# A three-block network on one core: expert results added to their tokens in DRAM by indexed DMAs

## The chip, the cores and the metric

The kernel runs on one core of one Trainium2 chip. The metric is the device time of one launch in microseconds (us): a median of 3149.73 over three runs (3148.05 to 3154.68). The profile is of one execution.

## The reference

A first block (recurrence, attention, feed-forward) is followed by a second block of two layers. Each layer of the second block ends in a mixture of experts with fixed capacity. The layer in question, the first, runs it for 512 latent tokens and, with the same weights, for 256 context tokens:

```python
def ec_moe(h, w_router, w_gate, w_up, w_down):
    bsz, n_tok, d = h.shape                       # d = 1024
    cap = EC_CAPACITY * n_tok // N_EXPERTS        # 64 of 512, 32 of 256; 16 experts
    aff = jax.nn.softmax(jnp.einsum('bnd,de->bne', h, w_router).astype(jnp.float32), axis=-1)
    g, idx = lax.top_k(jnp.swapaxes(aff, 1, 2), cap)
    xs = jax.vmap(lambda hb, ib: hb[ib])(h, idx)
    hid = jax.nn.silu(jnp.einsum('becd,edf->becf', xs, w_gate)) * jnp.einsum('becd,edf->becf', xs, w_up)
    ye = jnp.einsum('becf,efd->becd', hid, w_down) * g[..., None].astype(h.dtype)
    return jax.vmap(lambda yb, ib: jnp.zeros((n_tok, d), h.dtype).at[ib.reshape(-1)].add(yb.reshape(-1, d)))(ye, idx)
```

Around it, in each layer: `x = layer_norm(ALPHA * x + g2 * ec_moe(modulate(x, ...), ...))`, and the same for the context with its own modulation. A token can be chosen by several experts, so its line is a sum over them.

## The kernel before

`layer` calls `experts` (L2459) and then `norm_tiles` (L1883), once for each layer; both stand as stages with a crossing of all engines between them. All is float32. In `experts` the sixteen experts are taken as eight pairs (0 to 7). Their weights, 24 chunks of 1 MB for a pair, come through a ring of 8 slots and, in the first layer, 3 lent ones (the tile names `ring` and `tokens_b`); SP issues them in one order, each as soon as the chunk before it in its slot has been used (`Stream.issue`, L257).

`route` picks the tokens. `aff` holds the gates, `pos` the slot of each token at each expert. For each pair:

- `choose` (DVE) compares `pos` with a row of numbers and makes one-hot tables `choL`, `choC` (token by slot; L for latents, C for context). `list_slots` (PE, L2513 and L2516) multiplies them by the tokens' numbers, which gives the token of each slot; `take_index` (DVE) turns these into integers, and POOL fetches the tokens' lines from DRAM with two indirect DMAs (L2776, L2778). This runs two pairs ahead for the list and one pair ahead for the lines.
- `turn_rows` (PE) transposes the lines into PSUM, and ACT's `modulate` (L2744) scales them into `xsL`, `xsC`.
- `matrix` is one of the three products (gate, up, down) over 8 chunks: `latents` (L2558), then `context` (L2566), in groups of four chunks. The order on PE is: first product, second product, then what this text calls the **gap**, then the third product.
- In the gap PE does `turn_gates` (L2588, L2590), which transposes one-hot tables that DVE had multiplied by the gates (`gate`), `turn_hidden` (L2601), `turn_rows` for the next pair, `list_slots` for the pair after that, and `scatter` of the pair before (L2617): 12 products of the turned gate tables with that pair's results `yeL`, `yeC`, each added into `moe` (the tile name `tokens_a`) by DVE (L2706), with two PSUM banks in turn. The third product writes the banks that `turn_rows` filled, so it waits for ACT's `modulate`.
- After the third product DVE multiplies the result by the modulation row `growL`, `growC` (L2727, L2729), which gives `yeL`, `yeC`.

After pair 7 its scatter stands alone at the end, and `norm_tiles` starts with the statistics of `moe`, tile by tile (L1942). `moe` starts as ALPHA times x, made by ACT in `route`. The second layer has no context part (`C` and `G` are 0) and does not take this path.

## Time and profile before

| What | Value |
|---|---|
| median of three runs | 3149.73 us |
| the profiled execution | 3148.66 us, span 3146.8 us |
| PE busy | 2842.6 us, 90% of the span |
| PE weight loads | 1625.4 us, 52% |
| DVE / ACT / POOL busy | 1060.2 / 676.8 / 28.7 us |
| mean granted clock of PE | 0.948 |
| DMA | 569.42 MB, mean 181 GB/s |
| L2617, PE, the scatter's products (latents, both layers) | 256 records, 122.4 us busy |

Times are us from the start of the span. A float32 matmul has two records on PE. "x8" counts records or instructions merged into one row. PEclk is the granted clock of TensorE as a share of 2.4 GHz, so that 0.50 is 1.2 GHz. The DMA share is the mean busy share of the core's 16 DMA engines; it can pass 1 slightly in a short stretch. "Idle before" names what ended an engine's idle time. The busy time of overlapping records on PE is that of their union.

### The profile page before, as it was taken

Reading aid. Unit: us, or ns where it says so; the run is one execution under the profiler, and the core shown is the slowest. Engines: PE = TensorE matmul, PEld = TensorE weight load, DVE = VectorE, ACT = ScalarE, POOL = GpSimd, SP = SyncE. Lnnn points to the kernel's source line nnn. Section 1 sums busy time; section 2 is a strip of 40 time slices with the busy share of each in tenths; the row PEclk is TensorE's granted clock in tenths of the full one; section 3 lists DMA queues with packets and bytes.
Section 4 is the critical chain, followed back from the end, with each engine's and each line's share of the span. In section 5 each row is a group of like instructions: output and inputs, shape, how many; then the busy total and the mean of one; then the engine's idle time right before and its main releaser. Section 6 shows DMA issues by size and latency. Waiting matters only on the chain. (4 is left out here: it accounts for less than half of the span.)

```text
span 3146.8 us, 36640 instructions
## 1 busy us (share of the span) xinstructions
PE 2842.6 (90%) x15568; PEld 1625.4 (52%) x15568; DVE 1060.2 (34%) x2192; ACT 676.8 (22%) x1399; POOL 28.7 (1%) x45
## 2 busy tenths in 40 slices
PE   6998889899999689999489999999599995999996
PEld 5775655588864356774233333333277743433432
DVE  2513445132320227485501111111653753111213
ACT  3212225211100221471321111110211723100100
POOL 0010000000000000000000000000000000000000
PEclk9999979999999889999789999999799997999998
DMA  3227660122222121000368888887131004999995
GB/s 131 74 88 261 236 269 35 67 80 73 75 87 80 62 61 54 28 2 34 127 244 331 331 331 331 331 321 321 67 87 54 1 28 187 421 423 424 424 423 235
DMA packets 96904, 569.42 MB, mean 181 GB/s; under 512 B 24995, under 2 KB 25539, under 8 KB 31461
## 3 DMA queue, kind: packets, MB, share of 16 engines
q1 hardware_dynamic: 92852, 553.86, 45.1%
q0 software_dynamic: 3888, 13.22, 1.2%
q8 instruction: 123, 2.02, 0.3%
q14 instruction: 41, 0.33, 0.0%
HBM read 558.01 MB, written 9.03 MB: 180 GB/s over the span
## 5 line engine op out<-in xcount | busy, mean ns | idle before, releaser
L2558 PE MATMUL ps<-ring,xsL 128*64 128x512 f32 x1536 | 344.8, 600 | 9.6 <-ACTq L196 7.6
L1789 PE MATMUL ps<-hT,ring 128*128 128x257 f32 x1408 | 308.3, 381 | 1.6 <-PEq L1582 1.6
L1789 PEld LDWEIGHTS ps<-hT,ring 128*128 128x128 f32 x1408 | 268.0, 190 | 41.9 <-issue 1.9
L2558 PEld LDWEIGHTS ps<-ring,xsL 128*64 128x64 f32 x1536 | 109.7, 138 | 238.4 <-issue 221.2
L2721 DVE TENSOR_TENSOR hidL<-hidL,ps 128x1024 f32<-128x1024 f32 x16 | 19.5, 1221 | 515.6 <-PE ps L2566 312.9
L1752 PE MATMUL ps<-ring,actT 128*128 128x512 f32 x352 | 153.1, 598 | 7.0 <-PEq L1777 7.0
L2558 PE MATMUL ps<-ring,htL 128*64 128x512 f32 x616 | 140.0, 605 | 7.1 <-issue 3.8
L2751 ACT ACTIVATE hidL<-ps 128x1024 f32<-128x1024 f32 x16 | 16.4, 1023 | 603.3 <-PE ps L2566 368.2
L820 PE MATMUL ps<-hT,ring 128*128 128x264 f32 x640 | 143.8, 386 | 1.7 <-PEq L289 1.7
L2215 PE MATMUL ps<-tokens_a,ring 128*128 128x384 f32 x416 | 136.8, 491 | 4.9 <-PEq L384 4.9
L820 PEld LDWEIGHTS ps<-hT,ring 128*128 128x128 f32 x640 | 121.4, 190 | 23.2 <-issue 2.6
L2617 PE MATMUL ps<-yeL,gtL 128*128 128x512 f32 x256 | 122.4, 615 | 3.3 <-DVE yeC L2729 1.9
L2727 DVE TENSOR_TENSOR yeL<-ps,growL 128x1024 f32<-128x1024 f32 x16 | 19.6, 1224 | 289.3 <-PE ps L2566 171.3
L1752 PEld LDWEIGHTS ps<-ring,actT 128*128 128x128 f32 x352 | 67.5, 192 | 92.1 <-issue 92.1
L2215 PEld LDWEIGHTS ps<-tokens_a,ring 128*128 128x128 f32 x416 | 79.6, 192 | 60.9 <-issue 7.8
L2215 PE MATMUL ps<-tokens_b,ring 128*128 128x256 f32 (+1 forms) x416 | 103.6, 412 | 4.2 <-PEq L1909 4.2
L2333 DVE SCALAR_TENSOR_TENSOR z<-pad,cols,z 128x783 f32<-128x783 f32 (+1 forms) x120 | 101.9, 891 | 2.1
L601 ACT COPY probT<-ps 128x1280 f32<-128x1280 f32 (+5 forms) x80 | 81.1, 1013 | 69.2 <-PE ps L499 69.0
L2558 PEld LDWEIGHTS ps<-ring,htL 128*64 128x64 f32 x616 | 43.9, 139 | 99.2 <-issue 99.2
L2215 PEld LDWEIGHTS ps<-tokens_b,ring 128*128 128x128 f32 x416 | 80.8, 195 | 26.4 <-issue 5.3
L1834 DVE TENSOR_SCALAR conv<-raw,cols 128x512 f32<-128x512 f32 x44 | 19.4, 483 | 214.2 <-ACTq L196 214.2
L2566 PE MATMUL ps<-ring,xsC 128*32 128x512 f32 x768 | 88.8, 595 | 0.0
(492 smaller groups left out, 3893.9 us busy)
## 6 DMA issues: line engine op xcount, KB each, us to landing
ring<-in_w_exp SPq DMA_DIRECT2D x269, 1024.0 KB, 10.6
ring<-in_w SPq DMA_DIRECT2D x73, 1024.0 KB, 4.9
tokens_b<-in_w_exp SPq DMA_DIRECT2D x67, 1024.0 KB, 9.4
ring<-in_w_mod SPq DMA_DIRECT2D x48, 1024.0 KB, 5.2
h<-in_w_exp SPq DMA_DIRECT2D x16, 1024.0 KB, 14.5
tokens_a<-in_w_exp SPq DMA_DIRECT2D x16, 1024.0 KB, 15.2
lent<-in_w_exp SPq DMA_DIRECT2D x16, 1024.0 KB, 16.6
h<-in_x SPq DMA_DIRECT2D x2, 2048.0 KB
```

What stands on the lines that cost most here:

```text
L601: act.copy(probT[0:u["turn"], i % 2, 0:2 * nt, 0:u["n"]], T[0:u["turn"], 0:2 * nt, 0:u["n"]]).then_inc(pt_ready.sem, 1)
L820: mm = pe.matmul(ps[0:m, bank + h, 0:HALF1], lhs(c_), hT[:, c_, h * HALF1:(h + 1) * HALF1], start=c_ == 0, stop=c_ == KD - 1, skip_group_c ...
L1752: mm = pe.matmul(k.ps[:, 2 * j + half, :], actT[:, f, P * j:P * j + P], s[:, kk, half * BANK:(half + 1) * BANK], start=f == 0, stop=f == F ...
L1789: mm = pe.matmul(k.ps[:, 4 * (j % 2) + 2 * gv + h, 0:HALF], w(c_), hT[:, c_, FIRST + h * HALF:FIRST + (h + 1) * HALF], start=c_ == 0, stop ...
L1834: steps.free(dve.tensor_scalar(y, x, cw, None, ALU.mult))
L2215: mm = pe.matmul(ps[:, bank + h, 0:half], w(c_), uT[:, c_, h * half:(h + 1) * half], start=c_ == 0, stop=c_ == KD - 1, skip_group_check=True)
L2333: steps.free(dve.scalar_tensor_tensor(z[:, g, :], src, w, z[:, g, :], ALU.mult, ALU.add))
L2558: mm = pe.matmul(ps[HD * par:HD * par + HD, bank + half, :], lhsL(kk, par), weights(kk)[:, half, par, :], start=kk == 0, stop=kk == KD - 1 ...
L2566: mm = pe.matmul(ps[q:q + CAP_C, cbank, :], lhsC(kk, par), weights(kk)[:, half, par, :], start=kk == 0, stop=kk == KD - 1, skip_group_chec ...
L2617: pe.matmul(ps[:, MISC + half, :], lhsT, rhs, start=True, stop=True, skip_group_check=True).then_inc(scat.sem, 1)
L2721: dve.tensor_tensor(h[:, :], h[:, :], src, ALU.mult).then_inc(hid.sem, 1)
L2727: dve.tensor_tensor(yeL[:, :], psf[:, UB * BANK:(UB + 2) * BANK], growL[:, :], ALU.mult).then_inc(yes.sem, 1)
```

## The change

In the first layer the gate tables, their transposes and the scatter products are gone. The lists are made for more columns, so that each slot gets its token, its gate and, for the context, a second number: the product is with `table` (gates of both experts and the token's number) in place of the token's number alone, and some lists are made again for the odd expert, so that its results stand at partitions 0 to 63. `take_index` keeps integers and gates of all pairs. Behind the third product DVE multiplies by the slot's gate and the modulation row in one instruction. POOL adds the results to lines of `token_sums` in DRAM, four indirect DMAs for each pair: the even expert's latents and context, a wait for both, and the odd expert's (the two experts of a pair can have a token in common). `moe` is written to `token_sums` once at the start, and read back in six DMAs at the end; `norm_tiles` waits for each tile. The columns of PSUM that the context products write are ordered by expert now, which `growC` follows.

```diff
+                    if back and half == 0:
+                        dve.wait_ge(back[t].sem, back[t].of(16))
...
-            norm_tiles(k, ntq, x, summed=(moe, gb), to_next=(moe, by_channel_tile(b), k.mod[:, l + 1], 0))
+            norm_tiles(k, ntq, x, summed=(moe, gb), to_next=(moe, by_channel_tile(b), k.mod[:, l + 1], 0), back=k.back)
...
-                for t in range(NTL):
-                    pe.matmul(ps[:, MISC + 1, 256:257], choL[:, t, :, :].rearrange("p a s -> p (a s)"), c("token")[:, t:t + 1],
-                              start=t == 0, stop=t == NTL - 1, skip_group_check=True)
-                for t in range(2):
-                    mm = pe.matmul(ps[0:HD, MISC + 1, 257:258], choC[:, t, :, :].rearrange("p a s -> p (a s)"),
-                                   c("token")[:, NTL + t:NTL + t + 1], start=t == 0, stop=t == 1, skip_group_check=True)
-                mm.then_inc(listed.sem, 1)
+                if n >= 1:
+                    pe.wait_ge(indexed.sem, indexed.of(n))
+
+                def listing(m, at, lhs, lo, tiles, cols, first=0):
+                    for t in range(tiles):
+                        mm = pe.matmul(ps[first:first + m, MISC + 1, at:at + cols], lhs(t), table[:, lo + t, n, 3 - cols:3],
+                                       start=t == 0, stop=t == tiles - 1, skip_group_check=True)
+                    return mm
+                listing(P, 0, lambda t: choL[:, t, :, :].rearrange("p a s -> p (a s)"), 0, NTL, 3)
+                listing(HD, 3, lambda t: choL[:, t, 1, :], 0, NTL, 1)
+                for par in range(2):
+                    listing(CAP_C, 4, lambda t: choC[:, t, par, 0, :], NTL, 2, 1, CAP_C * par)
+                listing(P, 5, lambda t: choC[:, t, :, :, :].rearrange("p a h s -> p (a h s)"), NTL, 2, 3)
+                listing(HD, 8, lambda t: choC[:, t, 1, :, :].rearrange("p h s -> p (h s)"), NTL, 2, 1).then_inc(listed.sem, 1)
...
-                            q = HD * half + CAP_C * par
+                            q = HD * par + CAP_C * half
...
-                    if i == 1 and G:
-                        pe.wait_ge(indexed.sem, indexed.of(min(n + LEAD + 2, PAIRS)))
                     t, half = i // 2, i % 2
-                    if t < NTL:
-                        lhsT, rhs = gtL[:, n % 2, t, :], yeL[:, half * BANK:(half + 1) * BANK]
-                    else:
-                        b = slice(HD * half, HD * half + HD)
-                        lhsT, rhs = gtC[b, n % 2, t - NTL, :], yeC[b, :]
-                    pe.matmul(ps[:, MISC + half, :], lhsT, rhs, start=True, stop=True,
+                    pe.matmul(ps[:, MISC + half, :], gtL[:, n % 2, t, :], yeL[:, half * BANK:(half + 1) * BANK], start=True, stop=True,
...
-                turn_gates(n)
+                if not G:
+                    turn_gates(n)
                 turn_hidden(n)
                 if n + 1 < PAIRS:
                     if G:
                         turn_rows(n + 1)
                     else:
                         gather(n + 1)
-                pe.wait_ge(gts.sem, gts.of(n + 1))
-                if G and n + LEAD < PAIRS:
-                    list_slots(n + LEAD)
-                if n >= 1:
-                    scatter(n - 1)
+                if G:
+                    if n + LEAD < PAIRS:
+                        list_slots(n + LEAD)
+                else:
+                    pe.wait_ge(gts.sem, gts.of(n + 1))
+                    if n >= 1:
+                        scatter(n - 1)
...
+                for half in range(2 * C):
+                    is_slot(choC[:, :, :, half, :], pos, n, NTL, NT2, CAP_C)
...
+                got = ps[:, MISC + 1, :]
+                steps.free(dve.tensor_copy(index[0:HD, n, 0:3], got[0:HD, 2:5]))
+                steps.free(dve.tensor_copy(index[HD:P, n, 0:1], got[HD:P, 2:3]))
+                steps.free(dve.tensor_scalar(index[0:HD, n, 3:5], got[0:HD, 7:9], 2.0, c("low_half")[0:HD, :], ALU.mult, ALU.add))
+                for par in range(2):
+                    b = slice(HD * par, HD * par + HD)
+                    steps.free(dve.tensor_copy(gates[b, n, 0:1], got[b, par:par + 1]))
+                    steps.free(dve.tensor_copy(gates[b, n, 1:2], got[b, 5 + par:6 + par]))
                 steps.tell(indexed.sem)
+
+            def ended(n):
+
+                dve.wait_ge(used.sem, used.of(PAIR_CHUNKS * n + 24))
+                yL = psf[:, UB * BANK:(UB + 2) * BANK]
+                if G:
+                    if n >= 1:
+                        dve.wait_ge(summed.sem, summed.of(64 * n))
+                    dve.scalar_tensor_tensor(yeL[:, :], yL, gates[:, n, 0:1], growL[:, :], ALU.mult, ALU.mult).then_inc(yes.sem, 1)
+                    dve.scalar_tensor_tensor(yeC[:, :], ps[:, CU, :], gates[:, n, 1:2], growC[:, :], ALU.mult,
+                                             ALU.mult).then_inc(yes.sem, 1)
+                else:
+                    dve.tensor_tensor(yeL[:, :], yL, growL[:, :], ALU.mult).then_inc(yes.sem, 1)
...
+                steps.free(dve.tensor_copy(table[:, :, :, 0:2], aff[:, :, :].rearrange("p t (n a) -> p t n a", a=2)))
+                steps.free(dve.tensor_copy(table[:, :, :, 2], c("token").unsqueeze(2).to_broadcast([P, NT2, PAIRS])))
...
-                pool.wait_ge(sg["kept"].sem, sg["kept"].of(0))
-                for n in range(PAIRS):
+                def fetch(n):
                     pool.wait_ge(indexed.sem, indexed.of(n + 1))
                     if n >= 1:
                         pool.wait_ge(xs_turned.sem, xs_turned.of(PARTS * n))
                     pool.indirect_dma_start(rows[:, 0, :], None, k.rows[:, :],
-                                            bass.IndirectOffsetOnAxis(index[:, 0:1], 0)).then_inc(fetched.sem, 16)
+                                            bass.IndirectOffsetOnAxis(index[:, n, 0:1], 0)).then_inc(fetched.sem, 16)
                     pool.indirect_dma_start(rows[0:HD, 1, :], None, k.rows[:, :],
-                                            bass.IndirectOffsetOnAxis(index[0:HD, 1:2], 0)).then_inc(fetched.sem, 16)
+                                            bass.IndirectOffsetOnAxis(index[0:HD, n, 2:3], 0)).then_inc(fetched.sem, 16)
+
+                def sum_up(n):
+                    for par in range(2):
+                        b = slice(HD * par, HD * par + HD)
+                        if n >= 1 or par >= 1:
+                            pool.wait_ge(summed.sem, summed.of(32 * (2 * n + par)))
+                        pool.wait_ge(yes.sem, yes.of(PARTS * n + 1))
+                        pool.indirect_dma_start(k.sums[:, :], bass.IndirectOffsetOnAxis(index[0:HD, n, par:par + 1], 0), yeL[b, :],
+                                                None, compute_op=ALU.add).then_inc(summed.sem, 16)
+                        pool.wait_ge(yes.sem, yes.of(PARTS * n + 2))
+                        pool.indirect_dma_start(k.sums.rearrange("t (h d) -> (t h) d", h=2),
+                                                bass.IndirectOffsetOnAxis(index[0:HD, n, 3 + par:4 + par], 0), yeC[b, :], None,
+                                                compute_op=ALU.add).then_inc(summed.sem, 16)
+
+                pool.wait_ge(sg["kept"].sem, sg["kept"].of(0))
+                fetch(0)
+                pool.dma_start(k.sums.rearrange("(t p) d -> p t d", p=P), moe[:, :, :]).then_inc(begun.sem, 16)
+                pool.wait_ge(begun.sem, begun.of(16))
+                for n in range(1, PAIRS):
+                    fetch(n)
+                    sum_up(n - 1)
+                sum_up(PAIRS - 1)
+                pool.wait_ge(summed.sem, summed.of(64 * PAIRS))
+                for t in range(NT2):
+                    pool.dma_start(moe[:, t, :], k.sums[P * t:P * t + P, :]).then_inc(k.back[t].sem, 16)
```

PE from the end of the second product of pair 1 to its third product, before (`gatL`, `gatC` the gate tables, `rows` the fetched lines, `choL`, `choC` the one-hot tables, `htL` the hidden values for the third product):

```order
L2566 MATMUL ps<-ring,xsC 32x512 x16
L2588 MATMUL ps<-const,gatL 128x128 x4
L2590 MATMUL ps<-const,gatC 128x128 x2
L2601 MATMUL ps<-const,hidL 128x128 x8
L2601 MATMUL ps<-const,hidC 128x128 x4
L2524 MATMUL ps<-const,rows 128x128 x8
L2528 MATMUL ps<-const,rows 128x64 x8
L2513 MATMUL ps<-const_54,choL 128x1 x4
L2516 MATMUL ps<-const_54,choC 64x1 x2
L2617 MATMUL ps<-yeL,gtL 128x512 x8
L2617 MATMUL ps<-yeC,gtC 128x512 x4
L2558 MATMUL ps<-ring,htL 64x512 x4
```

and now:

```order
L2571 MATMUL ps<-ring,xsC 32x512 x16
L2601 MATMUL ps<-const,hidL 128x128 x8
L2601 MATMUL ps<-const,hidC 128x128 x4
L2536 MATMUL ps<-const,rows 128x128 x8
L2540 MATMUL ps<-const,rows 128x64 x8
L2522 MATMUL ps<-table,choL 128x3 x4
L2522 MATMUL ps<-table,choL 64x1 x4
L2522 MATMUL ps<-table,choC 32x1 x4
L2522 MATMUL ps<-table,choC 128x3 x2
L2522 MATMUL ps<-table,choC 64x1 x2
L2563 MATMUL ps<-ring,htL 64x512 x4
```

The turned gate tables (L2588, L2590) and the scatter (L2617) are gone from the gap, and the six matmuls of the list (4 and 2) have become sixteen (4, 4, 4, 2 and 2).

POOL's queue at the end of the stage, before (waits in brackets):

```order
L2776 DMA rows<-token_rows,index 128x1024 [waits xs_turned,indexed]
L2778 DMA rows<-token_rows,index 64x1024
L2776 DMA rows<-token_rows,index 128x1024 [waits xs_turned,indexed]
L2778 DMA rows<-token_rows,index 64x1024
L2506 UNCONDITIONAL_BRANCH
```

and now:

```order
L2787 DMA rows<-token_rows,index 128x1024 [waits xs_turned,indexed]
L2789 DMA rows<-token_rows,index 64x1024
L2798 DMA token_sums<-yeL,index 768x1024 [waits yes,summed]
L2801 DMA token_sums<-yeC,index 1536x512 [waits yes]
L2798 DMA token_sums<-yeL,index 768x1024 [waits yes,summed]
L2801 DMA token_sums<-yeC,index 1536x512 [waits yes]
L2798 DMA token_sums<-yeL,index 768x1024 [waits yes,summed]
L2801 DMA token_sums<-yeC,index 1536x512 [waits yes]
L2798 DMA token_sums<-yeL,index 768x1024 [waits yes,summed]
L2801 DMA token_sums<-yeC,index 1536x512 [waits yes]
L2815 DMA tokens_a<-token_sums 128x1024 [waits summed]
L2815 DMA tokens_a<-token_sums 128x1024 x5
```

The fetch for pair 7 stands ahead of the sums of pair 6, and the sums of pair 7 and the six reads of the tiles stand behind them. The fetch for each later pair stands behind all four sums of an earlier one in the same queue.

## Rows read from the trace of the kernel before

**Rows 1.** The page, part 2: mean GB/s of all DMA in 40 equal slices of the span.

```profile
GB/s 131 74 88 261 236 269 35 67 80 73 75 87 80 62 61 54 28 2 34 127 244 331 331 331 331 331 321 321 67 87 54 1 28 187 421 423 424 424 423 235
```

**Rows 2.** Stretches, us from the start: length, busy us and count by engine, PEclk, DMA share, GB/s.

```profile
1885.97:1966.63 80.66, 80.12 (x455) 27.17 (x454) 15.09 (x26) 9.15 (x22) 1.84 (x2) 1.00 0.81 323
1906.90:1949.50 42.60, 42.60 (x261) 12.59 (x257) 4.81 (x10) 1.51 (x2) 0.00 (x0) 1.00 0.99 397
1949.50:1955.20 5.70, 5.16 (x51) 4.66 (x47) 1.82 (x2) 4.02 (x10) 0.00 (x0) 1.00 1.01 425
1636.00:1641.00 5.00, 1.35 (x13) 1.25 (x12) 0.21 (x2) 4.88 (x15) 1.84 (x2) 0.90 1.02 429
```

**Rows 3.** Timeline, PE, gap of pair 4: start us, length, line, operation, records, [idle before].

```profile
1949.50 0.66 PE L2588 MATMUL ps<-const,gatL 128*128 128x128 f32 x4
...
1950.91 1.09 PE L2601 MATMUL ps<-const,hidL 128*128 128x128 f32 x8 [0.54 <-DVE hidL L2721]
...
1953.89 1.05 PE L2513 MATMUL ps<-const,choL 128*128 128x1 f32 x8
1954.87 0.39 PE L2516 MATMUL ps<-const,choC 128*64 128x1 f32 x4
1955.20 7.70 PE L2617 MATMUL ps<-yeL,gtL 128*128 128x512 f32 x16
...
1966.63 0.65 PE L2558 MATMUL ps<-ring,htL 128*64 128x512 f32 x2
```

**Rows 4.** Timeline, ACT, the same gap.

```profile
1956.47 2.47 ACT L2744 ACTIVATE xsC<-ps,mod 128x64 f32<-128x64 f32 x8
```

**Rows 5.** Timeline, PE, gap of pair 0 and the third product behind it.

```profile
1631.59 0.66 PE L2588 MATMUL ps<-const,gatL 128*128 128x128 f32 x4
...
1641.17 8.17 PE L2558 MATMUL ps<-ring,htL 128*64 128x512 f32 x24 [3.82 <-issue]
...
1665.15 1.08 PE L2558 MATMUL ps<-ring,xsL 128*64 128x512 f32 x4
```

**Rows 6.** Timeline, all engines, gap of pair 7.

```profile
2190.20 0.66 PE L2588 MATMUL ps<-const,gatL 128*128 128x128 f32 x4
...
2193.65 0.59 ACT L2763 COPY htC<-ps 128x512 f32<-128x512 f32 x1
...
2204.32 0.65 PE L2558 MATMUL ps<-tokens_b,htL 128*64 128x512 f32 x2
```

**Rows 7.** Timeline, all engines, opening of the stage.

```profile
1569.59 1.87 PE L2513 MATMUL ps<-const,choL 128*128 128x1 f32 x8 [1.82 <-DVEq L196]
...
1571.38 0.59 PE L2516 MATMUL ps<-const,choC 128*64 128x1 f32 x4
1572.01 0.16 DVE L2698 CAST index<-ps 128x1 int32<-128x1 f32 x1 [2.54 <-PE ps L2516]
...
1573.12 1.02 POOL L2776 DMA_INDIRECT rows<-token_rows,index  x1 [46.89 <-DVEq L196]
...
1574.44 0.92 POOL L2778 DMA_INDIRECT rows<-token_rows,index  x1 [0.30 <-issue]
...
1578.71 1.97 PE L2524 MATMUL ps<-const,rows 128*128 128x128 f32 x8 [2.89 <-DMA rows<-token_rows,index]
```

**Rows 8.** Timeline, DVE, end of the stage and the first row of the next.

```profile
2225.63 1.22 DVE L2727 TENSOR_TENSOR yeL<-ps,growL 128x1024 f32<-128x1024 f32 x1 [20.52 <-PE ps L2566]
...
2240.29 0.69 DVE L1942 BATCH_NORM_STATS2 stats<-tokens_a 128x6 f32<-128x512 f32 x1 [0.54 <-PEq L2506]
```

**Rows 9.** DMA issues (KB each, median us to landing), landing of token rows (DMA_INDIRECT), POOL issue.

```profile
lent<-in_w_exp SPq DMA_DIRECT2D x16, 1024.0 KB, 16.6
...
token_rows<-tokens_b POOLq DMA_DIRECT2D x6, 512.0 KB, 2.9
...
DMA to landing us min/median/max: 4.2/6.2/7.5
...
L2017 POOL DMA_DIRECT2D token_rows<-tokens_b x6 | 3.2, 532 | 1286.9 <-ACT tokens_b L2000 1286.9
```

More of the change, by code:

```diff
@@ L114, in constants @@
     first = [n for i, n in enumerate(parts) if i < first_only and n not in both]
-    second = ["iota", "token", "band"]
+    second = ["iota", "token", "low_half", "band"]
     inputs = [n for n in parts if n not in both and n not in first and n not in second]
@@ L1880, in by_channel_tile, with norm_tiles @@
     return buf[:, :].rearrange("p (k t) -> p k t", k=KD)
-def norm_tiles(k, nt, x, residual=None, summed=None, to_next=None, store=None, keep=None):
+def norm_tiles(k, nt, x, residual=None, summed=None, to_next=None, store=None, keep=None, back=None):
     nc, sg = k.nc, k.sig
@@ L2491, in experts @@
         rows = sb("rows", [P, 2, D])
-        index = sb("index", [P, 2], mybir.dt.int32)
+        index = sb("index", [P, PAIRS, 5], mybir.dt.int32)
+        gates = sb("gates", [P, PAIRS, 2])
+        table = sb("table", [P, NT2, PAIRS, 3])
     with ExitStack() as ctx:
         route(k, k.alloc(ctx), (xsL[:, :, :, :].rearrange("p k a s -> p (k a s)"), htL[:, :, :].rearrange("p k s -> p (k s)"),
-                                gtL[:, :, :, :].rearrange("p a t q -> p (a t q)"), hidL, yeL), uT, aff, pos, ntq, x, mod, moe, growL, growC)
+                                rows[:, 0, :] if G else gtL[:, :, :, :].rearrange("p a t q -> p (a t q)"), hidL, yeL), uT, aff, pos, ntq, x, mod, moe, growL, growC)
     if not C:
@@ L2540, in gather @@
                 mm.then_inc(xs_turned.sem, 1)
-                if C:
-                    for ch in range(KD):
-                        for t in range(2):
-                            mm = pe.matmul(ps[:, CU, ch * HD:(ch + 1) * HD], u[:, NTL + t, ch * P:(ch + 1) * P],
-                                           choC[:, t, :, :].rearrange("p a s -> p (a s)"), start=t == 0, stop=t == 1,
-                                           skip_group_check=True)
-                    mm.then_inc(xs_turned.sem, 1)
             def matrix(n, m, bank, cbank, lhsL, lhsC):
@@ L2584, in turn_gates @@
                     pe.wait_ge(added.sem, added.of(N_SC * (n - 1)))
-                if G:
-                    pe.wait_ge(indexed.sem, indexed.of(min(n + LEAD, PAIRS)))
                 for t in range(NTL):
                     mm = pe.transpose(ps[:, MISC, t * P:(t + 1) * P], gatL[:, t, :, :].rearrange("p a s -> p (a s)"), c("ident"))
-                for t in range(2 * C):
-                    mm = pe.transpose(ps[:, MISC + 1, t * P:(t + 1) * P], gatC[:, t, :, :, :].rearrange("p h a s -> p (h a s)"),
-                                      c("ident"))
                 mm.then_inc(gtr.sem, 1)
@@ L2684, in gate @@
                 is_slot(gatL[:, :, :, :], pos, n, 0, NTL, CAP_L)
-                for half in range(2 * C):
-                    is_slot(gatC[:, :, half, :, :], pos, n, NTL, NT2, CAP_C)
                 steps.join()
                 times_gate(gatL[:, :, :, :], n, 0, NTL, CAP_L)
-                for half in range(2 * C):
-                    times_gate(gatC[:, :, half, :, :], n, NTL, NT2, CAP_C)
                 steps.tell(gatd.sem)
@@ L2715, in _ @@
                     choose(n + LEAD)
-                gate(n)
+                if not G:
+                    gate(n)
                 for part in range(PARTS):
@@ L2784, in experts @@
     used.close(PAIR_CHUNKS * PAIRS)
-    for s in (choice, gatd, gtr, gts):
-        s.close(PAIRS)
+    choice.close(PAIRS)
     for s in (xs_turned, xs_, silu, hid, htr, hts, yes):
@@ L2792, in experts @@
         fetched.close(32 * PAIRS)
-    scat.close(N_SC * PAIRS)
-    added.close(N_SC * PAIRS)
+        begun.close(16)
+        summed.close(64 * PAIRS)
+    else:
+        for s in (gatd, gtr, gts):
+            s.close(PAIRS)
+        scat.close(N_SC * PAIRS)
+        added.close(N_SC * PAIRS)
 def route(k, sb, spare, uT, aff, pos, ntq, x, mod, moe, growL, growC):
@@ L2866, in _ @@
                 act.wait_ge(row_made.sem, row_made.of(i + 1))
-                steps.free(act.copy(*row_of(i)))
+                dst, src = row_of(i)
+                if row_jobs[i][0] == 0:
+                    steps.free(act.copy(dst, src))
+                else:
+                    for q in range(CAP_C * row_jobs[i][1], P, 2 * CAP_C):
+                        steps.free(act.copy(dst[q:q + CAP_C, :], src[q:q + CAP_C, :]))
             act.wait_ge(made.sem, made.of(2))
@@ L2990, in program @@
         k.rows = nc.dram_tensor("token_rows", (T2, D), F32).ap()
+        k.sums = nc.dram_tensor("token_sums", (T2, D), F32).ap()
+        k.back = [Signal(ctx.enter_context(nc.semaphore(f"back{t}"))) for t in range(NT2)]
         k.b_mod = sb("b_mod", [P, LAYERS, 6 * KD])
```

55 lines of the change are left out of this document (25 added, 30 removed).

## The prediction

> **What bounds the kernel now.** I read the page's slices first, then the stretches of the first expert stage (about 1568 to 2240 us), then the timeline of one gap. In the stage PE is busy 80.12 of 80.66 us from one third product to the next, at the full clock; DMA is busy 0.81 of that time, and 0.99 of it while the products run [rows 2]. So PE bounds the stage and the weight stream follows with some room. The second layer's experts later run at 421 to 424 GB/s for five slices [rows 1]; that stretch is bound by its transfers, which start from a full ring, so an earlier start moves it as a whole and a gain made before it isn't lost there.
>
> A pair's three products take 80.66 less the gap of 17.13 (1949.50 to 1966.63, [rows 3]), that is 63.5 us, or 21.2 each, and aren't touched. In the gap the scatter's products run from 1955.20 to 1966.63, 11.4 us [rows 3]. But PE couldn't have gone on at 1955.20: the third product needs ACT's scaling of the next lines, which ends at 1956.47 + 2.47 = 1958.94 [rows 4]. Pair 0 shows the gap without a scatter: 1631.59 to 1641.14, 9.55 us, with 3.82 us idle at its end [rows 5], for the same reason.
>
> **The gaps.** Pairs 1 to 5: 17.13 becomes 9.55, 7.58 less each, 37.9 in all. Turning the gate tables was hidden already: PE starts on the hidden values at 1950.91, released by DVE [rows 3], so removing it gives nothing. The longer list is hidden too. Warm, a record of the old list took 1.05/8 = 0.13 us at 128 columns and 0.39/4 = 0.10 at 64 [rows 3]; the new one has 12 records of 128, 12 of 64 and 8 of 32 (priced as 64), 3.5 us in place of 1.4, and from 1953.89 it ends near 1957.4, before ACT does. If this cover were gone it would cost 2.1 us a gap. Pair 6 has no list: from 1949.50 to 2190.20 [rows 3, 6] are three gap starts, 240.7 = 3 x 63.5 + 2 x 17.13 + 15.9, so its gap is 15.9 and saves 6.3. Pair 7 has neither lines nor list and waits for the hidden values alone: 2193.65 + 0.59 = 2194.24, and the product goes at about 2194.3 in place of 2204.32 [rows 6], 10.0 less. Pair 0 has no scatter to lose. Together **-54.2 us**.
>
> DVE's adds go with the scatter, and DVE waited anyway. The new scaling by the gate replaces a multiply of the same size, with 21 us before the next user of its PSUM banks.
>
> **The clock.** In pair 0 the granted share falls to 0.90 in 1636 to 1641 [rows 2], around the idle 3.82 us. The next 24 records take 8.17 us [rows 5], and the third product 1665.15 - 1641.14 = 24.0 us against 21.2: a fall to 1.2 GHz costs 2.8 us. In the gap of pair 4 the first 5.7 us hold transposes, a list and waits and stay at 1.00 [rows 2]; behind them comes the scatter with 512 columns. The change takes this scatter away in each gap. Between the last transposes and the third product there will then be 3.5 us of list with 1 to 3 columns and 1.5 us of idling (pair 6: about 5 us idle). No row shows a list this long, so the cost of a gap lies between 0 and 2.8 us. A saving is possible as well: pair 0 would get its 2.8 back if the list keeps the clock up. I take 2.8, as the state of PE (next to no columns for 5 us) is nearest to pair 0's, for pairs 1 to 6: **+16.8 us**. At 0 the forecast would be 3108, and with pair 0's gain 3106.
>
> The Trainium skill, TensorE: Matmul & The Clock Gate (PE-mode transpose), says that transposes don't count as busy for the clock in the way that matmuls do. The stretch of pair 4 that kept 1.00 through its transposes speaks against an immediate effect; by the page all gaps would dip, which is the sum as I take it.
>
> **The opening.** This runs on the critical path with PE at half clock. Ahead of the first list stand two copies for `table` (DVE, about 0.4 together, estimated from the small casts) and one more comparison (0.3). The old list took 1.87 + 0.59 = 2.46 us [rows 7]; at its 0.234 and 0.148 us a record the new one takes 5.8: +3.3. Seven conversions replace two, each at most 0.16 long and overlapped [rows 7]: +0.4. So the first fetch goes 4.4 later than 1573.12. Its lines would land near 1583.1 in place of 1578.71, but PE is then still at the second list, which has to stand ahead of the transposes: 4.7 later and 5.8 long, to 1583.9. **+5.2 us**; bounds 3 (lists as short as warm ones) to 8. The write of `moe` to DRAM (3 MB) stands behind the fetch, and its wait holds up only the second fetch, which has over 40 us.
>
> **The end of the stage.** Before: the last results from 2225.63, then 12 products and adds, and the next stage's first row at 2240.29 [rows 8]. Now: results of the latents at about 2226.95; POOL follows 0.3 later. A round is two issues, 1.02 + 0.30 to the second's start, and its landing. Two rounds are in series. Landing of an adding DMA isn't in the trace. A fetch of lines took 4.2 to 7.5 us [rows 9]; a sum reads its destination and writes it. Low end: 4.2, a round of 5.5. High end: 16.6, the landing of a 1 MB chunk in a long queue [rows 9], a round of 17.9. I take 7.5, the slowest fetch, so 8.8 a round. Then 2227.2 + 17.6 + 0.6 for two reactions; six reads at 0.53 on POOL [rows 9], 3.2, since the crossing waits for POOL's issuing; 0.5 for the crossing: 2249.1. The first tile, issued near 2245.4 and 2.9 landing [rows 9], is there by then. **+8.8 us**, bounds +2.2 and +27.
>
> The Trainium skill, DMA: Bandwidth & Descriptors (Anatomy of one DMA), fits a POOL-issued DMA with about 2 us plus its bytes at 436 GB/s. Its figure for a round's 0.39 MB would be 2.9 us of landing, and the whole sum would be 3116; the fetch's 4.2 at the least is above it.
>
> **In the middle of the stage** the sums are hidden in time: they start with a pair's end, and the next fetch in POOL's queue is needed 42 us (two products) and 3 later, against two rounds of 8.8 and a fetch of 7.5.
>
> Sum: -54.2 + 16.8 + 5.2 + 8.8 = -23.4. From the profiled execution's 3148.66 this gives **3125 us**; that execution is 1.1 below the median of the runs shown.
>
> **Rivals.**
>
> - A: the list keeps the clock up in most gaps. For: the 1.00 over 5.7 us of transposes and list. Against: pair 0, where the same work plus idling fell. 3148.66 - 54.2 + 5.2 + 8.8, with dips in pair 6 alone (+2.8) and pair 0's own gone (-2.8): 3108.
> - B, slower than before: the adding transfers hold the 16 DMA engines, and weights arrive late. DMA is busy 0.81 x 80.66 = 65.3 us a pair; the new pair is 73.1 us, which leaves 7.8 for two rounds. If a round holds the engines for H us, the deficit is 2H - 7.8 a pair, seven times, less about 18 us that seven chunks ahead in the ring cover once; the end of the stage costs 2H - 6.2. With -54.2 + 5.2 the total is zero at H = 8.0. At H = 10 it is +32: 3181. For: nothing in the trace shows what an addition costs an engine. Against: 0.39 MB at the 397 GB/s of [rows 2] is 1 us, 2 with the read of the destination.
> - C: the landing of a round is at its high end but leaves the engines free: 18 us more at the stage's end, 3143. It would look like a small gain or none.
> - D: the change doesn't shorten the gaps because another wait stands there, as the wait for the fetch behind the sums in POOL's queue. It would take rounds above 18 us each; that is B or C grown further.
>
> **Chances.** The forecast 0.48, A 0.27, C and mixtures near no change 0.13, B and D 0.12. The forecast's own range is 3115 to 3134. The range that should hold 8 in 10 is 3103 to 3146. About 0.2% (6 us) can be told from no change: faster 0.82, same 0.07, slower 0.11.
>
> **What would show it.** Right: gaps of pairs 1 to 6 of 9.5 us, ending with ACT's last scaling; PEclk of 0.5 for some us behind them; third products of 24.0 us; a fetch landing well ahead of its transposes; first row of the next stage about 23 us behind the last result. Wrong: idle time of PE before a product put down to a chunk; a gap set by the list or the fetch; first product and opening more than 8 us later; a last round beyond 18 us.

## The result, and the profile after

| What | before | after |
|---|---|---|
| median of four runs each | 3152.20 us (3148.05 to 3156.02) | 3132.36 us (3128.35 to 3137.96) |
| ratio, 95% interval | | 0.9939, 0.9917 to 0.9961 |
| the profiled execution | 3148.66 us, span 3146.8 | 3137.96 us, span 3136.1 |
| mean granted clock of PE | 0.948 | 0.932 |

The change saves 19.8 us of the median; the sum of the forecast was 23.4 less than the profiled execution (3148.66 to 3125). A later run of the same changed kernel gave 3129.0 us against 3151.27, ratio 0.9926 (0.9909 to 0.9942).

The profiled execution of after is the longest of its four. It reaches the changed stage late: the last result of the router's preparation (DVE's `pos`) starts at 1577.15 us, and at 1567.80 before. In the eight traces of the experiments below, whose first block is the same, it starts between 1566.30 and 1574.82 (1571.64 for the same kernel), so this is a spread between executions. The stage is therefore counted from the end of that `pos`, 0.26 us behind its start, in both traces, to the first row of the next stage. A gap is counted here from the start of DVE's `hidL`, which both kernels have, to the third product, and the third product of pair 7 to the start of `yeL`:

| Part of the stage, us | before | after | difference | forecast |
|---|---|---|---|---|
| `pos` to the first product (opening) | 18.25 | 22.47 | +4.2 | +5.2 |
| first and second product of pair 0 | 45.41 | 45.03 | -0.4 | 0 |
| eight gaps, counted from `hidL` | 124.1 | 70.0 | -54.1 | -54.2 |
| eight third products | 172.35 | 184.66 | +12.3 | +16.8 |
| `yeL` of pair 7 to the next stage's first row | 14.65 | 32.17 | +17.5 | +8.8 |
| whole stage | 672.23 | 651.84 | -20.4 | -23.4 |

The first two products of pairs 1 to 7 take 42.49 us each in both. With -20.4, the 9.35 us of late arrival and 0.3 behind the stage, 3148.66 becomes the 3137.96 measured.

The gap of pair 1 in the trace of after (timeline, PE: start, length, line, operation, records, idle before), which answers to [rows 3]:

```profile
1721.89 1.09 PE L2601 MATMUL ps<-const,hidL 128*128 128x128 f32 x8 [1.34 <-DVE hidL L2734]
1722.82 0.60 PE L2601 MATMUL ps<-const,hidC 128*128 128x128 f32 x4
1723.26 1.04 PE L2536 MATMUL ps<-const,rows 128*128 128x128 f32 x8
1724.22 0.71 PE L2540 MATMUL ps<-const,rows 64*128 64x64 f32 x8
1724.86 1.61 PE L2522 MATMUL ps<-table,choL 128*128 128x3 f32 x16
1726.40 1.16 PE L2522 MATMUL ps<-table,choC 128*32 128x1 f32 x16
1730.06 3.68 PE L2563 MATMUL ps<-ring,htL 128*64 128x512 f32 x8 [2.50 <-issue]
```

The scatter is gone, the list takes 1.61 and 1.16, and PE then idles 2.50 us for ACT's scaling. The next eight records take 3.68 us; eight take 1.94 at the full clock. The stretches of the same place (length, then busy us and count of PE, PEld, DVE, ACT, POOL, then PEclk, DMA share, GB/s) answer to [rows 2]:

```profile
1726.00:1730.00 4.00, 1.56 (x24) 1.43 (x23) 0.89 (x7) 3.79 (x12) 0.00 (x0) 0.74 1.01 422
1729.00:1733.00 4.00, 2.94 (x8) 1.11 (x10) 0.00 (x0) 0.92 (x4) 0.00 (x0) 0.50 1.01 422
1733.00:1737.00 4.00, 4.00 (x16) 1.29 (x14) 0.00 (x0) 0.00 (x0) 0.00 (x0) 0.79 0.21 84
```

The clock stands at 1.2 GHz (0.50) as the third product begins and comes back within 1733 to 1737. The end of the stage (timeline, all engines), which answers to [rows 8]:

```profile
2197.07 1.28 DVE L2705 SCALAR_TENSOR_TENSOR yeL<-ps,gates,growL 128x1024 f32<-128x1024 f32 x1 [23.46 <-PE ps L2571]
...
2199.10 1.41 POOL L2798 DMA_INDIRECT token_sums<-yeL,index  x1 [54.29 <-DVE yeC L2706]
2200.81 1.41 POOL L2801 DMA_INDIRECT token_sums<-yeC,index  x1 [0.30 <-issue]
2209.45 1.41 POOL L2798 DMA_INDIRECT token_sums<-yeL,index  x1 [7.22 <-DMA token_sums<-yeC,index]
2211.16 1.41 POOL L2801 DMA_INDIRECT token_sums<-yeC,index  x1 [0.30 <-issue]
2215.59 3.32 POOL L2815 DMA_DIRECT2D tokens_a<-token_sums  x6 [3.02 <-DMA token_sums<-yeC,index]
...
2229.24 1.28 DVE L1945 BATCH_NORM_STATS2 stats<-tokens_a 128x6 f32<-128x512 f32 x2 [30.22 <-PEq L2511]
```

POOL has issued its last read at 2218.91, and the next stage begins 10.33 us later. The core's DMA engines are at rest from about 2226 (DMA share 0.78 in 2224 to 2226, 0.01 in 2226 to 2227). DVE's wait is put down to PE's sequencer, the crossing; but PE had nothing to do since 2197, so the name is not that of the culprit.

The page's row of GB/s, which answers to [rows 1]:

```profile
GB/s 132 66 95 241 225 258 80 54 81 81 68 87 80 73 65 41 41 2 27 134 235 334 353 364 356 343 342 345 104 88 54 2 40 189 417 423 424 423 423 233
```

The stage's slices have 334 to 364 GB/s where they had 321 to 331: the same weights in less time, and the sums. The second layer's experts stream at 417 to 424 as before, so what the first layer gained was kept.

### The profile page after: what moved, and what is told of

Its sections match the earlier page's. It is cut to its first block and busy times, and to the rows that moved or that the text cites. A ratio compares the mean times of both kernels' runs of the same rounds, so it can differ in the third digit from the quotient of the medians.

```text
span 3136.1 us, 36393 instructions
## 1 busy us (share of the span) xinstructions
PE 2779.8 (89%) x15488; PEld 1614.1 (51%) x15488; DVE 984.7 (31%) x2098; ACT 671.0 (21%) x1385; POOL 80.4 (3%) x84
## 5 line engine op out<-in xcount | busy, mean ns | idle before, releaser
L2563 PE MATMUL ps<-ring,htL 128*64 128x512 f32 x616 | 149.6, 639 | 20.6 <-issue 17.4
L1810 ACT COPY raw<-ps 128x514 f32<-128x514 f32 x44 | 23.7, 590 | 269.8 <-PE ps L1790 269.8
L1926 PE MATMUL ps<-const,tokens_a 128*128 128x128 f32 x80 | 17.8, 397 | 70.0 <-ACT tokens_a L2003 70.0
```

The lines of the kernel that those rows point to most:

```text
L1810: steps.free(act.copy(halves(raw[:, j % 2, gv, :]), k.ps[:, b:b + 2, 0:HALF]))
L1926: mm = pe.transpose(k.ps[:, 4 + 2 * (s % 2) + c_ // 4, (c_ % 4) * P:(c_ % 4 + 1) * P], u[:, s, c_ * P:(c_ + 1) * P], k.c("ident"))
L2563: mm = pe.matmul(ps[HD * par:HD * par + HD, bank + half, :], lhsL(kk, par), weights(kk)[:, half, par, :], start=kk == 0, stop=kk == KD - 1 ...
```

## Experiments

Two open questions led them. The clock theory says that third products are longer because PE does too little in the gap; its rival, that the adding transfers slow them. The queue theory says that the end waits until POOL's DMA queue is empty; its rivals, that additions land slowly or that reading the tiles back takes the time. Each ratio is against runs of the kernel before on the same chip, and "stage" is counted as in the table above.

**after again.** The changed kernel, unchanged, as a base.

> The changed kernel as it is, timed again beside the others. The profile of its first execution stood 10 us late before the changed stage was reached, so the stage itself gained some 20 us there. Theory S (the stage alone changed; the 10 us ahead of it are the spread between executions, in the first block, which the change does not touch): a ratio to the kernel before of 0.992 to 0.995, pair periods of 75.1 to 75.7 us, and ahead of the stage an offset to the kernel before that varies from execution to execution. Rival U (something in the change slows the first block): the stage is reached 9 to 10 us late again.

3129.0 us (3125.02 to 3133.33), ratio 0.9926 (0.9909 to 0.9942). Stage 651.12 against 651.84, all parts within 0.8 us of the table's. The stage's numbers repeat far better than the whole time, so the parts below are read from stages.

**fill.** PE gets products without a use behind the list, in the gap of pairs 0 to 6.

```diff
+            def fill(count):
...
+                for _ in range(count):
+                    pe.matmul(ps[:, MISC, :], c("ident"), growL[:, 0:BANK], start=True, stop=True, skip_group_check=True)
...
+                        fill(2)
+                    elif n + 1 < PAIRS:
+                        fill(5)
```

> The changed kernel with matmuls that nobody reads (512 columns, onto the PSUM bank that the scatter used) in the gaps: two behind the list of pairs 0 to 5, 1.7 us in an idle time of 2.5, and five in the gap of pair 6, 4.3 us in 5.1. Theory K (the third products lose 2.3 us each because the clock falls while PE has next to no columns to stream): gaps stay at 9.5 us, PEclk stays at 1.00, third products go from 23.5 to 21.2 us, 7 x 2.3 = 16 us less than the changed kernel in the same call. If two fillers are too few against 2.7 us of list, the clock falls in part of the gaps and 5 to 10 us are gained. Rival D (the first matmuls of the third product are slow because of the additions' transfers or of the operands, not of the clock): no change within 2 us, or slower by what the fillers push out.

3123.85 us (3120.18 to 3127.65), ratio 0.9908 (0.9888 to 0.9927), 5.2 less than after again. Stage 641.31, 9.8 less: the third products fall from 184.65 to 171.65, the gaps grow by 1.9 in sum (those of pairs 2 and 4 by 0.6 and 1.0), and the end of the stage took 1.3 more in this trace. The timeline of PE in its gaps of pairs 1, 2 and 4 (L2616 are the added products):

```profile
1722.55 1.98 PE L2616 MATMUL ps<-growL,const 128*128 128x512 f32 x4
1725.11 1.94 PE L2563 MATMUL ps<-ring,htL 128*64 128x512 f32 x8 [0.58 <-issue]
...
1795.66 3.24 PE L2616 MATMUL ps<-growL,const 128*128 128x512 f32 x4
1798.83 4.05 PE L2563 MATMUL ps<-tokens_b,htL 128*64 128x512 f32 x16
...
1942.89 3.68 PE L2616 MATMUL ps<-growL,const 128*128 128x512 f32 x4
```

In pair 1 the fill runs at the full clock and so does the product behind it: 1.94 us for eight records in place of 3.68. In pairs 2 and 4 the same four records take 3.24 and 3.68 us. The granted clock of these places (columns as above):

```profile
1795.00:1796.00 1.00, 1.00 (x9) 0.92 (x9) 0.20 (x2) 0.88 (x4) 0.00 (x0) 1.00 1.00 410
1796.00:1797.00 1.00, 1.00 (x3) 0.29 (x2) 0.69 (x6) 1.00 (x5) 0.00 (x0) 0.63 1.04 434
1942.00:1943.00 1.00, 1.00 (x16) 0.95 (x11) 0.01 (x1) 0.88 (x4) 0.00 (x0) 1.00 0.99 418
1943.00:1944.00 1.00, 1.00 (x2) 0.48 (x3) 0.89 (x7) 1.00 (x4) 0.00 (x0) 0.51 1.01 426
```

The clock was whole through the list and fell behind it, about 0.6 and 0.1 us into the fill (estimates from these shares), with PE busy. It fell in the fill of pairs 0 and 5 as well (2.80 and 2.77 us), so in four gaps of seven. This holds the clock theory, with one amendment: the 2.5 us of idling at the end of the gap aren't needed. What stood ahead of the fall in pairs 2 and 4 were the 1.34 us idle before the hidden values, transposes and the list of 1 to 3 columns. No run takes these 1.34 us away, so it isn't shown that the list would be enough without them. The four falls are also why the third products gave 13.0 us in place of some 16.

**noscatter.** The kernel before, with the scatter products and DVE's adds of the first layer left out and nothing in their place, so that the experts' results reach no token.

```diff
-                if n >= 1:
+                if n >= 1 and not G:
                     scatter(n - 1)
...
-            scatter(PAIRS - 1)
+            if not G:
+                scatter(PAIRS - 1)
```

> The kernel before with the scatter's products and adds of the first expert layer left out and nothing in their place: the expert results of that layer are not added to the tokens. It keeps the short list, the gate tables and their transposes, and has no additions in DRAM. Theory K: gaps of 9.5 us like the changed kernel's, third products of about 23.5 to 24 us with PEclk at 0.50 behind each gap. Sum: -54.2 for the gaps, +14 to +17 for the clock, -12 for the last scatter: 48 to 52 us less than the kernel before, 28 to 31 less than the changed kernel (opening 4, end of the stage 20, next to nothing for contention). Rival D: third products of 21.2 us, since no additions run, and 62 to 66 us less than the kernel before.

3095.05 us (3089.91 to 3098.53), ratio 0.9821 (0.9805 to 0.9836), stage 618.75. Third products 184.86 in sum, as long as those of after (184.66), without a single addition, and gaps of 9.46 us (9.61 in pair 6) against 9.44. PE behind its gap of pair 4, and the stretches there:

```profile
1941.60 9.11 PE L2558 MATMUL ps<-ring,htL 128*64 128x512 f32 x32 [3.83 <-issue]
```

```profile
1942.00:1946.00 4.00, 4.00 (x12) 1.21 (x10) 0.00 (x0) 0.00 (x0) 0.00 (x0) 0.54 0.66 228
1946.00:1950.00 4.00, 4.00 (x20) 1.38 (x18) 0.00 (x0) 0.00 (x0) 0.00 (x0) 1.00 0.00 0
```

So the longer third products are the clock's doing and the rival falls. It also prices the new way of summing: after's stage is 33.1 us longer (651.84 less 618.75), of which 4.2 stand in the opening (the longer lists) and 29.8 at the end (32.17 against 2.40). In the 597 us between, 28 additions and the six fetches queued behind them cost nothing that shows.

**best.** The conclusions put together: after with the fill, with two fill products ahead of the very first product, and with pair 7 summed by products with one-hot gate tables, as before. The reads of the tiles then stand behind the sums of pair 6, while pair 7 is computed.

```diff
+                fill(2)
...
-            if not G:
-                pe.wait_ge(yes.sem, yes.of(PARTS * PAIRS))
+            pe.wait_ge(yes.sem, yes.of(PARTS * PAIRS))
+            if G:
+                scatter_last()
+            else:
...
-                sum_up(PAIRS - 1)
-                pool.wait_ge(summed.sem, summed.of(64 * PAIRS))
+                pool.wait_ge(summed.sem, summed.of(64 * (PAIRS - 1)))
```

> A version meant to beat both: the changed kernel, with the fillers of the other run, two fillers more ahead of the first product, and with pair 7 combined by products with gate tables as before (its tokens' lines are read back from DRAM during pair 7, when the sums of pair 6 have landed), so that no addition in DRAM stands at the end of the stage. By theory K: 16 us less than the changed kernel for the clock in the gaps, 1 to 3 for the first product, and at the end of the stage 14.7 us from the last result to the first row of the next in place of 22.4, 7 to 8 less. Sum: 24 to 27 us less than the changed kernel, about 43 to 46 less than the kernel before. If the reading back (3 MB) makes a chunk of the weights late, part of the 8 is lost in pair 7.

3101.89 us (3097.59 to 3110.46), ratio 0.9842 (0.9823 to 0.9862), stage 621.35. This beats both kernels: 49 us less than before and 27 less than after again, measured together. Of the 29.8 us of the stage (against after again), 13.5 come from the third products (171.12), 16.1 from the end (15.36) and 2.5 from the first product of pair 0, which now starts at the full clock; the gaps give 2.4 back. Its timeline (POOL, then DVE) at the end:

```profile
2136.91 3.33 POOL L2864 DMA_DIRECT2D tokens_a<-token_sums  x6 [7.64 <-DMA token_sums<-yeC,index]
...
2181.07 1.22 DVE L2740 TENSOR_TENSOR yeL<-ps,growL 128x1024 f32<-128x1024 f32 x1 [23.45 <-PE ps L2572]
...
2196.43 1.29 DVE L1945 BATCH_NORM_STATS2 stats<-tokens_a 128x6 f32<-128x512 f32 x2 [0.53 <-PEq L2512]
```

POOL has issued its last read 41 us ahead of the last result, and 15.36 us behind it the next stage starts, near before's 14.65 [rows 8]. This run moves several things at once; the next ones separate the end.

**sp reads.** The six reads of the tiles are issued by SP, behind the weights, with the same wait for all sums; nothing else is changed.

```diff
-                for t in range(NT2):
-                    pool.dma_start(moe[:, t, :], k.sums[P * t:P * t + P, :]).then_inc(k.back[t].sem, 16)
...
+            if G:
+                sp.wait_ge(summed.sem, summed.of(64 * PAIRS))
+                for t in range(NT2):
+                    sp.dma_start(moe[:, t, :], k.sums[P * t:P * t + P, :]).then_inc(k.back[t].sem, 16)
```

> The changed kernel with the six reads of the tiles at the end issued from SP in place of POOL, everything else the same. In the changed kernel the first row of the next stage stands 13.6 us behind POOL's first read. Theory Q (the crossing waits for POOL's queue to run empty, so for all six reads, however each tile is waited for): SP's crossing doesn't wait for its transfers, and the next stage starts when the first tile is there, about 3 us behind the first read; from the last result to the first row 22 to 23 us in place of 32, and 9 to 10 us less than the changed kernel, a ratio to the kernel before near 0.989 to 0.990. Rival R (the reads themselves land late, behind each other or because HBM has to finish the sums): the first row stays at 30 to 32 us behind the last result.

3125.04 us (3116.62 to 3128.15), ratio 0.9907 (0.9892 to 0.9922), stage 642.45. Its timeline at the end:

```profile
2193.47 1.28 DVE L2705 SCALAR_TENSOR_TENSOR yeL<-ps,gates,growL 128x1024 f32<-128x1024 f32 x1 [23.45 <-PE ps L2571]
...
2195.50 1.41 POOL L2798 DMA_INDIRECT token_sums<-yeL,index  x1 [54.40 <-DVE yeC L2706]
...
2205.81 1.41 POOL L2798 DMA_INDIRECT token_sums<-yeL,index  x1 [7.18 <-DMA token_sums<-yeC,index]
...
2211.72 2.93 SPq L2821 DMA_DIRECT2D tokens_a<-token_sums  x6
2216.30 1.28 DVE L1945 BATCH_NORM_STATS2 stats<-tokens_a 128x6 f32<-128x512 f32 x2 [20.89 <-PEq L2511]
```

```profile
2218.00:2222.00 4.00, 0.00 (x0) 0.00 (x0) 3.89 (x7) 0.20 (x1) 0.00 (x0) 0.50 0.82 328
```

The two rounds are nearly the same. But from the end of the last issue (2214.65) to the first row it is 1.65 us, with the transfers still running (the stretch has 328 GB/s and DVE at work), against 10.33 when POOL had issued them. `yeL` to first row is 22.83 in place of 31.45 to 32.17. The queue theory holds and both its rivals fall for this part, since neither the additions nor the reads had become quicker. The six reads landed like this, in after and then here:

```profile
DMA to landing us min/median/max: 4.0/6.5/8.3
DMA to landing us min/median/max: 3.7/6.2/8.6
```

So in after the first tile could have been there at about 2220 (an estimate: the first issue at 2215.59 and 4.0), and DVE started at 2229.24. The raw trace has one more record on POOL, which the views leave out: a DRAIN, in after from 2217.70 to 2228.89, 11.19 us, which ends 0.35 us before the first row. It stands in sp reads too, 4.05 us long, to 2215.95, and again 0.35 before the first row, though no DMA of POOL was under way any more. In best, where the reads share the DMA engines with weights and take up to 25.0 us to land, it takes 27.78: its length goes with the landing. So the 1.65 us are not the price of a bare crossing either: POOL still ended last.

The Trainium skill, DMA: Bandwidth & Descriptors (SWDGE vs HWDGE vs iDMA), gives plain transfers to SP or ACT and keeps POOL for adding and irregular ones. This pair of kernels agrees, with 8.6 to 9.3 us for it at this place.

**split fill.** best, with the fill cut in two: one product between the two parts of the list and one behind it, since the clock fell within the list.

```diff
+                if n >= LEAD:
+                    fill(1)
...
-                        fill(2)
+                        fill(1)
```

> The version meant to beat both, with one of the two fillers of each gap moved into the middle of the list. In the filled kernel the fillers were slow from their first record in two of the seven gaps (3.2 and 3.7 us in place of 2.0), so the clock had fallen during the list. Theory K: the clock needs columns, and a list of 2.7 us has next to none; cut into 1.6 and 1.2 us it holds in all gaps, the gaps go to 9.5 and the third products to 21.2 us, 2 to 3 us less than the version before it in the stage. If a list of any length lets the clock fall once it is in the wrong place, some gaps stay at 10 us or more and the stage stays within 1 us.

A miss. 3113.62 us (3109.27 to 3115.47), ratio 0.9879 (0.9864 to 0.9894), stage 632.33, 11.0 more than best: 5.2 in the third products, 4.2 in the gaps, 1.4 at the end. In best the clock falls in four of the first seven gaps (pairs 0, 1, 3 and 5, with 2.65 to 3.63 us for the fill's four records in place of 1.98); here it is five. Timeline of PE, gap of pair 1 and then of pair 2 (L2518 the fill):

```profile
1716.09 1.66 PE L2518 MATMUL ps<-growL,const 128*128 128x512 f32 x2
1717.69 1.86 PE L2528 MATMUL ps<-table,choC 128*32 128x1 f32 x16
1719.47 2.07 PE L2518 MATMUL ps<-growL,const 128*128 128x512 f32 x2
...
1791.85 1.13 PE L2518 MATMUL ps<-growL,const 128*128 128x512 f32 x2
1792.91 1.16 PE L2528 MATMUL ps<-table,choC 128*32 128x1 f32 x16
1794.00 1.12 PE L2518 MATMUL ps<-growL,const 128*128 128x512 f32 x2
```

Pair 2 keeps its clock, with two records at 1.13; in pair 1 they take 1.66, so it fell about the start of the fill. The clock can fall behind the 1.34 us of idling, transposes and the first part of the list alone. The simple form of my theory, that more products closer together keep it up, isn't enough; what decides in which gap it falls stays open.

**plain.** after, with `compute_op=ALU.add` taken from the four indirect DMAs: lines are overwritten, not added to, with the same indices and the same bytes written, so the results aren't sums. One execution.

```diff
-                                                None, compute_op=ALU.add).then_inc(summed.sem, 16)
+                                                None).then_inc(summed.sem, 16)
...
```

> The changed kernel with plain indexed writes in place of additions: a token's line gets the result written last, so the experts' results are not summed. Same bytes written, no reading of the destination. In the changed kernel a round (latents and context) takes 10.2 to 11 us from the first issue to the next round's. Theory A (an addition costs the read of its destination and more issuing): issues of 0.9 to 1.0 us in place of 1.4, and rounds of 5.5 to 7 us, so 8 us less at the end of the stage; pair periods as before, since the rounds are hidden there. Rival P (rounds are set by fixed latency, not by adding): rounds of 9 us or more.

3124.24 us, stage 647.64. POOL's first two rounds, here and then in after:

```profile
1669.16 0.93 POOL L2798 DMA_INDIRECT token_sums<-yeL,index  x1 [77.00 <-DVE yeL L2705]
...
1677.70 0.89 POOL L2798 DMA_INDIRECT token_sums<-yeL,index  x1 [6.36 <-DMA token_sums<-yeC,index]
```

```profile
1679.83 1.49 POOL L2798 DMA_INDIRECT token_sums<-yeL,index  x1 [77.91 <-DVE yeL L2705]
...
1690.34 1.40 POOL L2798 DMA_INDIRECT token_sums<-yeL,index  x1 [7.29 <-DMA token_sums<-yeC,index]
```

An issue takes 0.89 in place of 1.41 us in the median and this round 8.5 in place of 10.5, of which 1.0 us is the two issues; the end of the stage is 28.92, 2.5 to 3.3 us shorter. Most of a round is what an indirect write costs, whether it adds or not.

**short list.** after, with the matmuls for the odd expert's second copies left out of the list, so that their indices aren't right; sizes and counts of the DMAs stay. `take_index` reads its numbers from the lists that are left. One execution.

```diff
-                listing(HD, 3, lambda t: choL[:, t, 1, :], 0, NTL, 1)
-                for par in range(2):
-                    listing(CAP_C, 4, lambda t: choC[:, t, par, 0, :], NTL, 2, 1, CAP_C * par)
...
-                listing(HD, 8, lambda t: choC[:, t, 1, :, :].rearrange("p h s -> p (h s)"), NTL, 2, 1).then_inc(listed.sem, 1)
...
```

> The changed kernel with six matmuls in the list in place of sixteen: the odd expert's results go to the tokens of the even one, and some gates are left from other slots, so that the sums are wrong in value and not in work. Expected: the opening (end of the routing's copy to the first product) goes from 22.5 back to 20 us, since two lists at half clock stood in it, one ahead of the fetch and one beside it; gaps unchanged at 9.5 us, as ACT ends them; third products between 23.2 and 24 us as before, since a shorter list leaves more idling in its place. If the list were what costs the clock, third products would come down to 21.2.

3127.5 us, stage 648.68. The opening is 20.39, 2.1 less. In the gaps the list takes 1.6 us and PE idles 3.71 (the eight records behind it take 3.68, as in after), and the third products sum to 183.92, 0.7 less than r1's 184.65: list or idling, the clock falls just the same.

## Why the prediction was right, and where it was wrong

- *The gaps, -54.2.* Right to 0.1 us in sum. From `hidL` the gaps of pairs 0 to 6 are 9.44 us and that of pair 7 is 3.96. Each ends with PE idling for ACT's last scaling, 2.50 us, and 5.13 in pair 6, which has no list. ACT's scaling was indeed what stood next behind the scatter.
- *The clock, +16.8.* Right in mechanism; the price of 2.8 us a gap was too high. Third products of pairs 1 to 6 take 23.47 down to 23.16 us against 21.18, which is 2.1 us each and 12.5 in all; the fall for every one of the seven gaps, and for no reason of DMA, is shown by noscatter. Pair 0's, from which the price was taken, was 23.97 before and 23.78 after: with the longer list its idle time shrinks from 3.82 us [rows 5] to about 2.5, and it loses nearly as much. Each later pair loses a little less than the one before it, with the same instructions in its gap; why was not tried.
- *The opening, +5.2.* 4.2, though the order of events was not as written. Either of the two first lists takes 4.6 us (2.81 and 1.84, overlapping), not 5.8: with 2.81 for the twelve records of 128 columns, which is the price taken, the twenty narrower ones took 0.09 each, not 0.148. Warm, it takes 2.7 and not 3.5, so it left PE idle for 2.5 us rather than 1.5. The second list was to end behind the landing of the lines; in after it ends at 1590.89, and the transposes wait 1.38 us more for the lines. So the 4.2 are 3.4 for a later fetch (POOL's issue 8.71 us behind the start of `pos`, 5.32 before; 4.4 forecast) and 0.8 more from its issue to the transposes. The end of the second list and the transposes (PE):

```profile
1589.05 1.84 PE L2522 MATMUL ps<-table,choC 128*32 128x1 f32 x16
1592.28 1.97 PE L2536 MATMUL ps<-const,rows 128*128 128x128 f32 x8 [1.38 <-DMA rows<-token_rows,index]
```

- *The end of the stage, +8.8.* The failed step, with 17.5. The two rounds, 17.6 and 0.6 for reactions, are 16.5 in fact (2199.10 to 2215.59), but not of one length: 10.35 and 6.14, the second with the DMA engines half busy (share 0.50 in 2210 to 2216). POOL's first issue waits for `yeC`, 0.75 us behind `yeL` and not 0.3. The six reads are 3.3 (forecast 3.2). What was mis-sized is "0.5 for the crossing", with its ground "since the crossing waits for POOL's issuing": it took 10.33, since it waits for what POOL has issued to land, and 3 to 4 us more (the DMA engines are at rest from about 2226, the first row is at 2229.24). sp reads shows it: 1.65 us there. The value lies within the bounds (+2.2 and +27), but these were made for the landing of the sums, so they held it for another reason. Its profile test, a first row about 23 us behind the last result, showed the miss: 32.17.
- *The middle of the stage.* Right: noscatter differs from after by less than 1 us outside the two ends. The fetches took longer than the 7.5 us allowed for them, 11.5 and 12.7 in the median (6.1 and 6.2 before) and 14.1 at most, and the 42 us hid that too. In after PE's waits in the stage (total us, times, longest) name no chunk at all:

```profile
PE ps L2563 <- issue: 19.9, 7, 5.1
PE ps L2601 <- DVE hidL L2734: 10.8, 8, 1.3
PE ps L2563 <- ACTq L197: 4.6, 1, 4.6
PE ps L2563 <- ACT htC L2775: 1.2, 1, 1.2
```

- *Rivals.* A (the clock stays up) is refuted by every gap. B (the additions hold the DMA engines) is refuted by the rows above. A round takes 10.5 us, more than the H of 8.0 that B needed, but as latency: the engines aren't held for it, or chunks would have been late. C asked for a round of 17.9; the longest is 11.2 (1755.73 to 1766.96). D would have shown as gaps above 9.5.

That the sum was off by 3.0 us only is luck, since misses of opposite sign met: 8.7 us too little at the end; 4.5 and 1.0 too much for the clock and the opening, and 0.4 in pair 0 (with 0.1 the other way in the gaps). Of the other 4.4 us from 3125 to 3132.36, 3.5 are before's median over the four runs, 3152.20, above its profiled execution; 0.9 is rounding and spread.

The Trainium skill, DMA: Bandwidth & Descriptors (Anatomy of one DMA), with its 2 us and bytes, would have had 2.9 us of landing for a round (an estimate from its figures). The trace of after has 4.6, 8.5 and 9.1 us as least, median and greatest for the additions of the latents, and 4.1, 8.6 and 9.3 for those of the context, so the measurement decides against it for indirect additions:

```profile
L2798 POOL DMA_INDIRECT token_sums<-yeL,index x16: 1402/1410/1817, 1679.8 to 2209.4; - x16
...
DMA to landing us min/median/max: 4.6/8.5/9.1
```

## What to carry to other kernels

Sums by indirect adding DMAs are free where 40 us of other work cover two rounds of 10, and dear at a stage's end: do the last piece by the old way and read back while it is computed. Before a crossing, count what POOL's queue still has in flight and issue plain transfers from another queue. Where filler work is cut out of PE's queue, price the clock for the product behind it, 2.1 us each here, and count whether the gap saved is worth more.

## What the runs showed of the hardware that had not been expected

- A crossing of all engines waits for DMAs issued by POOL (9.6 to 10.7 us behind the last of six 512 KB reads, in after, after again, fill, plain and short list) and not for those of SP (1.65 us).
- An indirect adding DMA takes 1.41 us to issue, a plain indirect write 0.89, and lands in 8.5 or 8.6 us in the median (latents, context) against 7.6 or 7.5.
- The clock fell to 1.2 GHz with PE busy, after 1.34 us of idling, then transposes and a list of 1.6 to 2.7 us (fill, pairs 2 and 4; split fill, pair 1), in some gaps and not in others that hold the same instructions.
